# Prompt attention on both heads of a row tile at once, and six activation tiles rounded earlier

## What is computed

```
def dilated_group_attn(q, k_all, v_all, offset, dil, n_keys):   # 3 groups: window 128/512/2048, dilation 1/4/16
    s = einsum('bqhd,bqjhd->bqhj', qb, kb) * hd ** -0.5          # 8 heads of 64
    s = where(valid, s, -inf);  m = max(s, -1);  p = exp(s - m);  den = sum(p, -1)
    o = einsum('bqhj,bqjhd->bqhd', p / den, vb);  lse = m + log(den)
...
    w = softmax(stack(lses, 0), axis=0);  o = einsum('gblh,gblhd->blhd', w, stack(outs, 0))

def swiglu(h, w_in, w_out):                                      # D_FF = 2816
    gu = h @ w_in
    return (silu(gu[..., :D_FF]) * gu[..., D_FF:]) @ w_out
```

## Time and profile before

| | |
|---|---|
| median of 3 runs | 2214.02 us (2211.15 to 2217.9) |
| profiled execution, its own time | 2214.46 us |
| its span | 2212.7 us |
| granted TensorE clock, mean of the span | 0.941 of 2.4 GHz |
| busy: PE, DVE, ACT, POOL | 89%, 48%, 32%, 7% of the span |

### The profile page before, as it was taken

The page is one execution under the profiler, slowest core; times in us unless marked ns, Lnnn a source line. Parts: engine busy times, 40 slices in busy tenths (PEclk is TensorE's granted clock), DMA queues, the critical chain, the costliest instruction groups (busy, mean ns, idle before and its releaser), DMA issues.

```text
span 2212.7 us, 35064 instructions
## 1 busy us (share of the span) xinstructions
PE 1961.1 (89%) x14822; PEld 1780.5 (80%) x14822; DVE 1060.1 (48%) x1819; ACT 697.5 (32%) x1179; POOL 160.9 (7%) x205
## 2 busy tenths in 40 slices
PE   5657799977999999999999999677888799999998
PEld 4556688854999999998998977552775599999998
DVE  6669623454443334326887147631465253333422
ACT  4323214332343333224443234230333243332311
POOL 1135100001000000002000100131000000000000
PEclk9778899998999999999999989898999799999999
DMA  5533414517233322221223210196423433233131
GB/s 147 146 67 47 76 59 152 171 39 257 67 86 86 95 76 90 86 72 55 63 77 110 94 40 1 49 286 199 133 77 116 164 83 95 76 94 97 64 97 49
DMA packets 219528, 218.01 MB, mean 99 GB/s; under 512 B 16964, under 2 KB 202768, under 8 KB 217360
## 3 DMA queue, kind: packets, MB, share of 16 engines
q1 hardware_dynamic: 201296, 142.61, 22.7%
q0 software_dynamic: 17120, 70.13, 9.7%
q10 hardware_dynamic: 992, 3.54, 0.5%
HBM read 200.23 MB, written 11.83 MB: 96 GB/s over the span
## 4 chain that ended last, share of the span: by engine, by line
PE 62%; DVE 6%; DMA 5%; ACT 1%; POOL 1%; issue 1%; DVEq 0%; POOLq 0%; ACTq 0%; SPq 0%
PE ps L1522 47%; PE ps L2271 3%; PE ps L2453 2%; DMA arena<-in_cache_swa_k_dram 2%; DMA arena<-in_cache_swa_v_dram 2%; PE ps L2438 2%; DVE arena L593 1%; PE ps L1310 1%; DMA arena<-in_cache_mem_v_dram 1%; PE ps L2428 1%; DVE ring_r L2190 1%; PE ps L2260 1%; PE ps L2641 1%; PE ps L1816 1%; PE ps L2442 1%
## 5 line engine op out<-in xcount | busy, mean ns | idle before, releaser
L1522 PE MATMUL ps<-h_ffn_r,w_parts_r 128*128 128x272 f32 x3328 | 557.3, 288 | 1.5 <-DVE w_parts_r L1515 1.5
L1522 PEld LDWEIGHTS ps<-h_ffn_r,w_parts_r 128*128 128x128 f32 x3328 | 469.8, 189 | 2.1 <-DVE w_parts_r L1515 1.9
L1522 PE MATMUL ps<-h_lo_r,w_parts_r 128*128 128x272 f32 x1920 | 379.3, 288 | 0.0
L1522 PEld LDWEIGHTS ps<-h_lo_r,w_parts_r 128*128 128x128 f32 x1920 | 294.8, 188 | 0.0
L1509 ACT ACTIVATE w_parts_r<-ring 128x2048 fp32r<-128x2048 f32 (+1 forms) x76 | 128.5, 1691 | 344.9 <-PE ps L1522 344.8
L1515 DVE TENSOR_TENSOR w_parts_r<-ring,w_parts_r 128x2048 fp32r<-128x2048 f32 (+1 forms) x76 | 152.8, 2011 | 119.9 <-ACT w_parts_r L1509 119.0
L1619 DVE TENSOR_TENSOR arena<-ps,rstd 128x272 f32<-128x272 f32 (+1 forms) x176 | 69.2, 436 | 294.0 <-PE ps L1522 294.0
L571 DVE TENSOR_TENSOR arena<-arena 128x32 f32<-128x32 f32 (+7 forms) x238 | 135.6, 579 | 24.6 <-ACT arena L1895 17.2
L1522 PE MATMUL ps<-act_lo_r,w_parts_r 128*128 128x272 f32 x704 | 146.3, 289 | 0.0
L593 DVE RECIPROCAL arena<-arena 128x544 f32<-128x544 f32 (+4 forms) x43 | 115.8, 2694 | 16.0 <-ACT arena L1885 7.6
L1522 PEld LDWEIGHTS ps<-act_lo_r,w_parts_r 128*128 128x128 f32 x704 | 111.6, 190 | 0.0
(11 more groups left out here) (395 smaller groups left out, 3391.0 us busy)
## 6 DMA issues: line engine op xcount, KB each, us to landing
ring<-in_ffn_w_in_dram SPq DMA_DIRECT2D x88, 512.0 KB, 5.0
ring<-in_ffn_w_out_dram SPq DMA_DIRECT2D x16, 1408.0 KB, 6.2
ring<-in_attn_w_qkv_dram SPq DMA_DIRECT2D x18, 1024.0 KB, 5.1
ring<-in_mem_w_kv_dram SPq DMA_DIRECT2D x16, 1024.0 KB, 6.0
arena<-in_cache_mem_k_dram POOLq DMA_DIRECT2D x16, 1024.0 KB, 6.4
arena<-in_cache_mem_v_dram POOLq DMA_DIRECT2D x16, 1024.0 KB, 6.7
ring<-in_mem_w_q_dram SPq DMA_DIRECT2D x8, 1024.0 KB, 6.7
ring<-in_mem_w_o_dram SPq DMA_DIRECT2D x8, 1024.0 KB, 9.5
```

The costliest lines, as they stand in the source:

```text
L1522: last = [t.matmul(outs[h], wp[:, k, cs], x[:, half(h)], start=start and n == 0, stop=stop and n == 2) for h in range(2)]
```

## The change

A step of the prompt attention is now both heads of a row tile, 16 steps in all. Scores of the two heads alternate, matmul by matmul, between partitions 0 to 63 and 64 to 127 of the array's rows and write to different banks; value products alternate between output partitions 0 to 63 and 64 to 127 of one bank. A step uses eight banks: three for twelve transposes, four for scores, one for the result. The first head's weights are still scaled by VectorE, the second head's by ScalarE; ScalarE reads two of the three banks of transposes and VectorE one; one reciprocal and one copy to `hT` serve both heads. `pT2` holds one step instead of two. In the SwiGLU the rounded copies and remainders of tiles 0 to 5 are made in the two last units, three in each, and the split of the second output weight piece follows tile 6.

```diff
@@ plan_swa
-            for n in range(SH * 4 + 2):
+            for n in range(SH * 2 + 2):
                 if n >= 2:
-                    item("ap", n - 2, 0)
-                    item("ap", n - 2, 1)
-                if n < SH * 4:
-                    item("as", n, 0)
-                    item("as", n, 1)
+                    for i in range(3):
+                        item("ap", n - 2, i)
+                if n < SH * 2:
+                    for i in range(2):
+                        for e in range(2):
+                            item("as", n, e, i)
                 if n >= 2:
                     item("ao", n - 2)
@@ a_ffn, unit_step
+                if final:
+                    for k in range(MR * u, MR * u + MR):
+                        L.need("act_made", 2 * FT * l + 2 * k + 2)
+                        L.did(nc.scalar.activation(ahi(l, k), act[:, k], ACT.Copy), "a_hi")
@@ a_ffn
-            for k in range(FT):
-                if k == 0:
+            for k in range(2 * MR, FT):
+                if k == 2 * MR:
                     L.need("act_made", 2 * FT * (l + 1))
                 L.did(nc.scalar.activation(ahi(l, k), act[:, k], ACT.Copy), "a_hi")
-                if k == 5:
+                if k == 2 * MR:
                     a_split(L, l, (0, 0, 1))
@@ v_ffn: unit_step calls v_act_low(k) for the same tiles, after its v_split
+            def v_act_low(k):
+                L.need("a_hi", FT * l + k + 1)
+                L.did(nc.vector.tensor_tensor(alo[:, k], act[:, k], ahi(l, k).bitcast(F32), ALU.subtract), "a_lo")
@@ pe_attn
+            rows_ = [slice(64 * e, 64 * e + 64) for e in range(2)]
             for n in range(NA + 2):
+                m = n - 2
                 if n >= 2:
+                    for i in range(12):
+                        if i % 4 == 0:
+                            b = fill(pe, ("ap", m, i // 4))
+                        if i % 6 == 0:
+                            pe.wait_ge(S(("ap_first", "ap_second")[i // 6]), m + 1)
+                        ins = t.transpose(b[:, P * (i % 4):P * (i % 4) + P],
+                                          sc2[:, 2 * (m % 3) + i // 6, P * (i % 6):P * (i % 6) + P], ident[:])
+                        if i % 4 == 3:
+                            filled(("ap", m, i // 4), ins)
                 if n < NA:
+                    f, r = n // 4, n % 4
+                    b = [fill(pe, ("as", n, e, 0)) for e in range(2)]
+                    for e, q in enumerate(rows_):
+                        filled(("as", n, e, 0), t.matmul(b[e][:, :], q2[q, 0, f, P * r:P * r + P], k2[q, 0, f, 0:SEQ],
+                                                         start=True, stop=True))
+                    b = [fill(pe, ("as", n, e, 1)) for e in range(2)]
                     for g in (1, 2):
+                        for e, q in enumerate(rows_):
+                            ins = t.matmul(b[e][:, P * (g - 1):P * g], q2[q, g, f, P * r:P * r + P],
+                                           k2[q, g, f, P * r:P * r + P], start=True, stop=True)
+                            if g == 2:
+                                filled(("as", n, e, 1), ins)
                 if n >= 2:
+                    f, r = m // 4, m % 4
+                    for i in range(3):
+                        landed(pe, ("ap", m, i))
                     b = fill(pe, ("ao", m))
                     for c in range(6):
+                        for e, q in enumerate(rows_):
+                            hc = slice(SD * (2 * f + e), SD * (2 * f + e) + SD)
+                            vv = Vt[:, c, 0, hc] if c < 4 else Vt[:, r, c - 3, hc]
+                            ins = t.matmul(b[q, 0:P], vv, pT2[:, P * (6 * e + c):P * (6 * e + c) + P], start=(c == 0),
+                                           stop=(c == 5), skip_group_check=True)
                     filled(("ao", m), ins)
@@ v_attn
+                if 1 <= n <= NA:
+                    x = 16 * ((n - 1) % 3)
+                    L.need("aexp", 2 * n)
+                    L.recip(sa[:, x + 10:x + 12], sa[:, x + 8:x + 10], sem="a_inverse")
+                    i = 2 * ((n - 1) % 3)
+                    L.ts(sc2[:, i], sc2[:, i], sa[:, x + 10:x + 11], None, ALU.mult, sem="ap_first")
                 if n >= 2:
+                    b = full(L, ("ap", m, 2))
+                    free(L, ("ap", m, 2), v.tensor_copy(pT2[:, 8 * P:], b[:, :]))
...
+                    for e in range(2):                       # masks, maxima, negated maximum, as before, per head
...
                 if n >= 2:
                     b = full(L, ("ao", m))
+                    free(L, ("ao", m), v.tensor_copy(hT[:, m // 4, slice(m % 4, SEQ, 4)], b[:, 0:P]))
@@ a_attn
+                if 1 <= n <= NA:
+                    L.need("a_inverse", n)
+                    L.did(s.activation(sc2[:, i], sc2[:, i], ACT.Copy, scale=sa[:, x + 11:x + 12]), "ap_second")
                 if n >= 2:
+                    for i in range(2):
+                        b = full(L, ("ap", m, i))
+                        free(L, ("ap", m, i), s.activation(pT2[:, 512 * i:512 * i + 512], b[:, :], ACT.Copy))
                 if n < NA:
+                    for e in range(2):
+                        L.need("anmx_ready", 2 * n + e + 1)  # then the exponential of head e, as before
```

More of the change, by code:

```diff
@@ L1614, in unit_step @@
                     v_split(L, l, (0,), i + 1)
+                if final:
+                    for k in range(MR * u, MR * u + MR):
+                        v_act_low(k)
                 k = 2 * i + u
@@ L2056, in hybrid_step @@
         W2 = Space(arena, AR, u0)
-        sc2 = W2.take(3 * 6 * P, "p (i n) -> p i n", i=3)
-        pT2 = W2.take(2 * 6 * P, "p (i n) -> p i n", i=2)
+        sc2 = W2.take(6 * 6 * P, "p (i n) -> p i n", i=6)
+        pT2 = W2.take(2 * 6 * P)
         VS = 7 * SW
@@ L2407, in a_first_h @@
                 a_square(L, "fo0", 2, m)
-        def step(n):
-            return n // 8, (n % 8) // 2, n % 2
-        NA = SH * 4
+        NA = SH * 2
         def pe_attn(pe):
@@ L2421, in pe_attn @@
                     landed(pe, ("qkv", u, i))
+            rows_ = [slice(64 * e, 64 * e + 64) for e in range(2)]
             for n in range(NA + 2):
+                m = n - 2
                 if n >= 2:
[L2424 to L2433, removed]
-                if n < NA:
[L2435 to L2440, removed]
-                    for g in (1, 2):
-                        ins = t.matmul(b[:, P * (g - 1):P * g], q2[q, g, f, P * r:P * r + P],
-                                       k2[q, g, f, P * r:P * r + P], start=True, stop=True)
-                    filled(("as", n, 1), ins)
+                    for i in range(12):
[7 more added lines that the diff above has]
+                            filled(("ap", m, i // 4), ins)
@@ L2459, in v_attn @@
             for n in range(NA + 2):
-                if n >= 2:
[L2461 to L2469, removed]
+                m = n - 2
+                if 1 <= n <= NA:
[4 more added lines that the diff above has]
+                    L.ts(sc2[:, i], sc2[:, i], sa[:, x + 10:x + 11], None, ALU.mult, sem="ap_first")
+                if n >= 2:
+                    b = full(L, ("ap", m, 2))
+                    free(L, ("ap", m, 2), v.tensor_copy(pT2[:, 8 * P:], b[:, :]))
                 if n < NA:
-                    f, r, e = step(n)
                     x = 16 * (n % 3)
+                    r = n % 4
                     if n >= 3:
-                        m = items[("ap", n - 3, 1)]
-                        L.e.wait_ge(S(f"bank_full{m % 8}"), m // 8 + 1)
+                        full(L, ("ap", n - 3, 2))
                     elif n == 0:
@@ L2478, in v_attn @@
                         L.settle()
[L2479 to L2486, removed]
+                    for e in range(2):
+                        i = 2 * (n % 3) + e
+                        b = full(L, ("as", n, e, 0))
+                        free(L, ("as", n, e, 0), v.tensor_tensor_reduce(
+                            sc2[:, i, 0:512], b[:, :], M0[:, P * (3 - r):P * (7 - r)], 1.0, -3e38, ALU.add, ALU.max,
+                            sa[:, x + e:x + e + 1]))
+                        b = full(L, ("as", n, e, 1))
+                        free(L, ("as", n, e, 1), v.tensor_tensor_reduce(
+                            sc2[:, i, 512:768], b[:, 0:256], M12, 1.0, -3e38, ALU.add, ALU.max, sa[:, x + 2 + e:x + 3 + e]))
+                        L.tt(sa[:, x + 4 + e:x + 5 + e], sa[:, x + e:x + e + 1], sa[:, x + 2 + e:x + 3 + e], ALU.max)
+                        L.ts(sa[:, x + 6 + e:x + 7 + e], sa[:, x + 4 + e:x + 5 + e], -SS, None, ALU.mult, sem="anmx_ready")
                 if n >= 2:
-                    m = n - 2
-                    f, r, e = step(m)
                     b = full(L, ("ao", m))
-                    h = slice(64 * e, 64 * e + 64)
-                    free(L, ("ao", m), v.tensor_copy(hT[h, f, slice(r, SEQ, 4)], b[h, 0:P]))
```

(28 more changed lines are left out.)

7 lines of the change are left out of this document (removed).

## The result

The changed kernel takes 2158.8 us (median of 4; before 2212.59 in the same session), ratio 0.9758, 95% interval 0.9734 to 0.9782. The profiled execution took 2158.91 with a span of 2157.1, against 2212.7.

The account below looks back on a forecast made before the run. TensorE was taken to bound the attention before, VectorE's loop after. From 2214.46, 32.3 for attention and 8.2 for two SwiGLUs come off, giving 2174.0 us; its own range 2166 to 2183, widened to 2190.

Parts of the forecast that it names:

- Overlap of halves: Attention, TensorE: scores and value products of both heads overlap fully, transposes do not; 4.57 us a double step instead of 7.52.
- Rival (a): Attention: TensorE overlaps less than full; 2187 if scores do not overlap, 2206 if nothing does; chance 0.15 for the family.
- VectorE's loop as the bound: Attention: VectorE's operations plus its wait for the exponential set a double step of 5.4 us, lower bound 4.70.
- TensorE is just ahead, by 0.2 to 0.3: Attention: next scores are there at t + 7.7, VectorE asks at t + 7.94; TensorE idles 0.8 a double step.
- The beginning runs at 1.2 GHz, as before, for about 20 us: Attention start: slow clock for about 20 us, with first-pair scores 3.0 instead of 1.5, transposes 3.2, value products 2.9.
- The walk: Attention start: the first four double steps followed at the slow clock put the fourth maximum 25 us after the start.
- The end of the stage: Attention: from the last maximum to the last copy, 9.4 us.
- Rival (b): Attention: TensorE's gaps keep the clock at 1.2 GHz, 9.14 us a double step, 2232 in all; chance 0.05 for slower.
- Rival (c): After the attention: the cache DMAs take back the attention's gain, ending near 2205; chance 0.03.
- SwiGLU: Both SwiGLUs: moving six tiles ahead saves net 4.1 us each (3.0 + 1.7 - 0.6), 8.2 in all.
- Tile 7: SwiGLU: tile 7's remainder is the next late one, making TensorE wait 0.6 us.
- the 1.7 for the clock: SwiGLU: the 5.6 us at clock 0.80 and 0.61 after the first output product go, worth 1.7 us.

Follow-up runs that it names:

- values_serial: The changed kernel with value products made head after head and scores still alternating; 2166.68 us, ratio 0.9801.
- one_small_op: The changed kernel with the maximum of the two maxima and its scaling in one VectorE operation per head instead of two; 2156.14 us, ratio 0.9762.
- third_copy_act: The changed kernel with ScalarE instead of VectorE copying the third bank of transposes; 2166.4 us, ratio 0.9812.
- early_serial: The changed kernel with the first four of sixteen double steps head after head, the others alternating; one run, 2173.2 us.
- attn_only: The attention part of the change alone, SwiGLU as in the kernel before; 2171.44 us, ratio 0.981.
- after_again: The changed kernel once more, nothing altered; 2159.47 us, ratio 0.9769.
- before_again: The kernel before the change once more, nothing altered; one run, 2203.97 us.
- both_serial: The changed kernel with scores and value products both made head after head, without alternation; 2178.88 us, ratio 0.9839.

## Why the prediction was wrong, step by step

**The sum of terms.** The forecast was 40.5 less, the spans differ by 55.6. These 15.1 us are: attention 40.1 instead of 32.3, SwiGLU 7.9 (4.07 and 3.84) instead of 8.2, and 7.5 in stretches that the change does not touch. The steps that failed are thus the length of the slow start (5.0 us of the attention's 7.8), the size of VectorE's loop (2.7), and a term that the sum put at nothing without a reason, the unchanged stretches (7.5, half of the miss).

**Overlap of halves: right.** Scores, value products and transposes were put at 1.50, 1.45 and 1.62 for a double step; they take 1.50, 1.46 and 1.46. The 77% taken from the Trainium skill's page "TensorE: Matmul & The Clock Gate", Part 3, would have made it 5.45 by the prediction's estimate; the trace is at 4.42, nearer to the ideal. Rival (a), "nothing overlaps", was priced at 7.52, as if the pieces of the earlier trace rows were pure work, though each holds something per change of kind as well; grouped, it would be about 7.2 (the estimate above). What nobody had priced is that two blocks of different halves overlap at their border without alternation, which is worth 0.87.

**VectorE's loop as the bound: right, mis-sized.** Put at 5.39, measured 5.18. The parts that do not depend on the one before start earlier than their lengths in the earlier trace rows suggest: the copy 0.54 after the scaling (1338.55 to 1339.09) instead of 0.63, the second head 1.33 after the first instead of 1.42. Twelve double steps make 2.7 us of it. "TensorE is just ahead, by 0.2 to 0.3" was right, and it was ahead by 0.13 to 0.19, as `values_serial` and `one_small_op` show; `third_copy_act` shows what happens when that is used up. The rule of the Trainium skill's page "TensorEngine Tiling (Array Packing)", section "PSUM Bottleneck", is only half of it here: the trace agrees that a reader of PSUM became the bound (VectorE's loop, 5.18 us), but relieving VectorE of one PSUM read made the double step longer (5.45 in `third_copy_act`).

**"The beginning runs at 1.2 GHz, as before, for about 20 us": the step of the attention that failed most.** The fourth double step's maximum was ready 20.0 us after the start and not 25. The time at 1.2 GHz was 6.6 us. I took one trace's length for a property of the stage, while it varies with the execution and goes with the order of the matmuls. It makes 5.0 of the 7.8 us. The walk itself came near: in `early_serial`, with 20.1 us at 1.2 GHz and no alternation in those four, the fourth maximum came 25.8 us after the start. The end of the stage was put at 9.4 and took 9.2.

**Rival (b), a clock that stays low, did not come.** The clock is 1.00 in every window from 1292 to the end of the stage, with TensorE busy for 3.3 of 4 us in most of them. In four other traces of the new grouping (`attn_only`, `after_again`, `one_small_op`, `third_copy_act`) it fell once more, for 3.4 us near the end of the stage, where nothing is left between TensorE's waits but transposes and value products. In `after_again`:
```profile
1366.53 1.67 PE L2465 MATMUL ps<-arena 128*64 128x128 f32 x24 [2.19 <-ACT arena L2517]
1368.12 2.82 PE L2439 MATMUL ps<-ident,arena 128*128 128x128 f32 x12
```
The twelve transposes take 2.82 there and 1.53 in the trace after, so this costs some 1.4 us; it is why the stage of `after_again` is longer (92.2 to 91.4) though its start was faster. Rival (c) did not come either.

**SwiGLU: right.** 4.1 each was forecast, 4.07 and 3.84 came. Tile 7 was the late one as named (0.5 instead of 0.6), and the clock did not fall. But the 1.7 for the clock belong to one execution. In `before_again` the clock stayed at 1.00 behind the wait of 3.00, and TensorE came to tile 6 before the weight split was done:
```profile
877.21 0.52 PE L1522 MATMUL ps<-h_lo_r,w_parts_r 128*128 128x272 f32 x2 [0.71 <-DVE act_lo_r L1634]
```
Against that trace the change is worth 3.5 us for each SwiGLU.

**What the range left out.** It was built from costs of instructions alone. The unchanged stretches differ too: before the first SwiGLU's last multiplication 869.4 and 873.5 us in `before_again` and before, 868.7 to 874.4 over all fourteen traces; from the end of the attention to the second one 642.3, 644.9 and 645.7 in the three traces with the old attention, 636.0 to 647.0 in the eleven with a new one. Most of that lies in the samples' attention, which waits for cache DMAs: its last key transpose comes 68.1, 68.7 and 68.7 us after the stage with the old attention and 64.8 and 65.8 in the two traces of the changed kernel. Of the nine others with a new attention eight have 65.4 to 67.1, and `both_serial` has 71.8. Against `before_again` (span 2202.2) and `after_again` (2155.5) the account is attention 33.1, SwiGLU 7.0, behind the attention 7.7, and -1.1 in all other stretches together. So 33 to 40 us for the attention and 7 to 8 for the SwiGLU are shown, where 32.3 and 8.2 were forecast: between two executions with equally short slow starts the forecast of both parts was right within 1.2 us each; whether the change also shortens the DMA-bound stage by some 3 us, or the executions only differ, is open. No run isolates it.

## What to carry to other kernels

Price a regrouping apart from an overlap: run the new grouping without the alternation, and check in its trace that the overlap is really gone. Here half of what TensorE's period lost came without alternation, but 0.87 us of that half were still overlap, at the borders between blocks, and only 0.33 went with fewer changes between kinds of matmul. Where a pipeline reaches over two steps, add up the longest way across both, and check which operation is common to it and to the busiest engine's loop; only that one is worth shortening. Before a range is given, look how long unchanged stretches and slow-clock stretches take in more than one execution.

## What the runs showed of the hardware

Twelve value records of one half take 1.45 us between other kinds of matmul, 24 in two blocks of twelve take 2.38, and 24 alternating 1.46. Records of different halves overlap even at the border between two blocks that do not alternate: scores take 2.47 for what took 3.00, 0.44 of it by such an overlap. TensorE stayed at 1.2 GHz for 14 to 20 us, almost always busy, in four of five traces in which nothing alternates at the start of the stage, and for 3 to 7 us in all nine in which halves alternate there, though it has gaps in those. The fifth differs in that its clock fell 6 us into the stage and not at its start.
